# Layer norm sums that begin on VectorE and run under the weight blocks, taps written out, and earlier attention steps, in a three-layer block on one core

## The chip, the cores and the metric

The kernel runs on one core of a Trainium2 chip. The metric is the device time of one execution in microseconds (us), the median of three runs. TensorE is called PE, VectorE DVE, ScalarE ACT, GpSimd POOL and SyncE SP, as in the profile.

## The reference

A stream x of 256 rows and 2048 channels passes a convolution layer, a gated linear recurrence (HGRN), a sliding-window attention and a feed-forward layer. The change touches the first and the third. Of the convolution layer this is computed (`E` = 2048, 31 taps):

```python
def conformer_conv(h, w_in, dw, dw_b, ln_g, ln_b, w_out):
    u = h @ w_in
    a, b, z = jnp.split(u, 3, axis=-1)
    v = a * jax.nn.sigmoid(b)
    v = depthwise_conv(v, dw) + dw_b          # 31 taps along the rows, channel by channel
    v = jax.nn.silu(layer_norm(v, ln_g, ln_b))
    return (v * jax.nn.silu(z)) @ w_out
```

The layer norm takes mean and variance over the 2048 channels of a row. The attention has 32 query heads of 64 channels and 4 key and value heads, rows in two blocks of 128, a window of 128 rows, and a learned sink in each head's softmax.

## The kernel before, in words

**Weights.** All products run over weight blocks: 656 blocks of 256 x 512 fp32, loaded by SP into four slots `raw`. ACT rounds a block into `w_hi` (line 637), DVE (line 977) or POOL (line 345) subtracts to get `w_lo`, and PE then makes 12 products 128x512 with it (lines 376 to 378: hi by hi, lo by hi, hi by lo, for two 128-row halves of the block and two row blocks of x). With four slots ACT can round block n only when PE has used block n - 4. POOL makes the `w_lo` of blocks 16 to 95, because DVE is then busy with the taps.

**Order.** Each engine has its own program in which `stream` walks the blocks of a phase. `Hooks` is a table written by hand: after block i of the phase (on PE after its products, on ACT after its `w_hi`, on DVE after its `w_lo`) the engine does the steps that were put at tick i. Semaphores join the engines. The phases that matter here are `conv_ab` (4 groups of 16 blocks, 0 to 63), `conv_z` (32 blocks), `conv_out` (32), and later `kv_q` (40) and `att_out` (32), whose ticks are counted on from `kv_q` as 40 and up.

**Convolution.** For each group j of 512 channels, ACT moves a and sigmoid(b) to `atok` and `sg`, POOL multiplies them (`v_out`), PE turns the result (`v_turn`), ACT copies it into the padded `vpad` (`pad_copy`), and DVE does 31 taps for each of four channel tiles of 128 channels (`taps`, line 1032; 124 instructions a group, in a hardware loop over j). Each tap waits for the tap before the last one, since two tiles alternate.

**Layer norm.** After the last block of `conv_z`, PE turns the last quarter of z (`z_turn(3)`), adds the channels with 16 products by a matrix of 1/2048 (`mean`, line 435), DVE subtracts the mean, ACT squares, PE adds with 16 more products (`variance`, line 442), ACT takes the root, DVE the reciprocal (line 1057), and then scaling, SiLU, the gate by z, `y_hi` and `y_lo` follow for four quarters of the channels. The first product of `conv_out` needs the first `y_lo`.

**Attention.** The 32 heads go in four groups g of 8. With e = 16 + 8g: q is normalised and rotated on DVE (`rope`), turned on PE (`q_turn`), scored on PE in two halves of four heads (`scores`), masked on DVE (`masked`, line 1306), the row maxima are taken for all eight heads at once (`maxima`, lines 1313 to 1321), ACT takes the exponentials (`exps`, lines 901 and 902), PE turns the probabilities (`turn_p`, line 557), ACT copies them (`p_copy`), PE multiplies by v (`mix_v`, lines 566 to 568), DVE scales (`finish`), PE turns again (`y_turn`), and ACT and DVE make `y_hi` and `hy_lo` (`y_out_hi`, `y_low`). Block 52 on PE needs `hy_lo` of group 3.

## Time and profile before

| what | value |
|---|---|
| median of three runs | 2094.3 us (2093.97 to 2095.67) |
| the profiled execution, its own time | 2096.97 us |
| its span | 2095.2 us |
| PE busy | 2016.1 us, 96% |
| DVE busy | 1264.4 us, 60% |
| ACT busy | 1064.5 us, 51% |
| POOL busy | 203.3 us, 10% |
| granted clock of PE, mean | 0.982 of full |

The span is the part that the trace covers; the time of the execution holds 1.8 us more. A busy PE here is one with a product under way; how fast it goes is seen in the clock and in the distance from one start to the next.

### The profile page before, as it was taken

How to read it: one execution, taken by the hardware profiler on the slowest of the kernel's cores; microseconds unless marked ns; L12 is line 12 of the kernel's file. 1: busy time of each engine (PE TensorE's matmuls, PEld its weight loads, DVE VectorE, ACT ScalarE, POOL GpSimd, SP SyncE). 2: the span in 40 equal slices, each digit the busy share in tenths (PEclk: the TensorE clock that was granted, in tenths of full speed). 3: DMA queues.
4: the chain of work that ended last, by engine and by line, in shares of the span. 5: the costliest groups of instructions: out<-in, count | busy, mean ns of one | idle time of the engine just before them, and what ended most of it. 6: DMA issues, size and time to landing. Idle time of an engine off the chain costs nothing.

```text
span 2095.2 us, 26893 instructions
## 1 busy us (share of the span) xinstructions
PE 2016.1 (96%) x9504; PEld 1677.0 (80%) x9504; DVE 1264.4 (60%) x1694; ACT 1064.5 (51%) x1350; POOL 203.3 (10%) x92
## 2 busy tenths in 40 slices
PE   7999997999999999999999987999999999999999
PEld 6777776888888888878887776788888888888887
DVE  5499965543877777795657653454544545444443
ACT  6444445455758585874555553454444434443332
POOL 0888840000000000000000000000000000000000
PEclk9999998999999999999999997999999999999999
DMA  8565542566545454545564332465666665666664
GB/s 287 180 181 180 173 150 91 186 196 182 159 140 163 131 172 138 161 131 171 168 205 131 101 100 71 157 194 171 201 190 190 190 190 172 199 195 194 194 192 161
DMA packets 182855, 352.81 MB, mean 168 GB/s; under 512 B 11616, under 2 KB 12000, under 8 KB 182752
## 3 DMA queue, kind: packets, MB, share of 16 engines
q1 hardware_dynamic: 181184, 350.27, 54.5%
q10 hardware_dynamic: 1568, 1.23, 0.2%
q8 instruction: 57, 0.93, 0.2%
q14 instruction: 46, 0.38, 0.1%
HBM read 349.36 MB, written 2.10 MB: 168 GB/s over the span
## 4 chain that ended last, share of the span: by engine, by line
PE 87%; DVE 5%; ACT 4%; issue 2%; DVEq 1%; POOL 0%; ACTq 0%; DMA 0%; SPq 0%
PE acc L376 26%; PE acc L378 26%; PE acc L377 26%; PE T L477 3%; PE T L358 2%; ACT w_hi L637 1%; DVEq L969 1%; DVE w_lo L977 1%; PE T L557 1%; POOL w_lo L345 0%; PE T L566 0%; PE T L567 0%; PE T L568 0%; PE T L435 0%; PE T L487 0%
## 5 line engine op out<-in xcount | busy, mean ns | idle before, releaser
L977 DVE TENSOR_TENSOR w_lo<-raw,w_hi 128x1024 fp32r<-128x1024 f32 x576 | 699.8, 1224 | 635.6 <-ACT w_hi L637 627.7
L637 ACT ACTIVATE w_hi<-raw 128x1024 fp32r<-128x1024 f32 x656 | 683.1, 1058 | 548.0 <-PE acc L378 519.2
L376 PE MATMUL acc<-w_hi,h_hi 128*128 128x512 f32 x1888 | 748.3, 396 | 23.3 <-DVE h_lo L989 13.4
L378 PE MATMUL acc<-w_hi,h_lo 128*128 128x512 f32 x1888 | 739.3, 392 | 0.0
L377 PE MATMUL acc<-w_lo,h_hi 128*128 128x512 f32 x1888 | 739.0, 391 | 0.0
L376 PEld LDWEIGHTS acc<-w_hi,h_hi 128*128 128x128 f32 x1888 | 357.2, 189 | 99.2 <-DVE h_lo L989 13.4
L378 PEld LDWEIGHTS acc<-w_hi,h_lo 128*128 128x128 f32 x1888 | 356.7, 189 | 75.3
L377 PEld LDWEIGHTS acc<-w_lo,h_hi 128*128 128x128 f32 x1888 | 357.0, 189 | 71.2
L345 POOL TENSOR_TENSOR w_lo<-raw,w_hi 128x1024 fp32r<-128x1024 f32 x80 | 189.7, 2405 | 84.0 <-ACT w_hi L637 84.0
L1032 DVE SCALAR_TENSOR_TENSOR T<-vpad,feat,T 128x256 f32<-128x256 f32 x464 | 183.6, 483 | 0.7 <-DVE T L1032 0.6
L376 PE MATMUL acc<-w_hi,y_hi 128*128 128x512 f32 x384 | 157.3, 410 | 20.5 <-DVE y_lo L982 11.3
L377 PE MATMUL acc<-w_lo,y_hi 128*128 128x512 f32 x384 | 154.4, 402 | 0.0
L376 PE MATMUL acc<-w_hi,f_hi 128*128 128x512 f32 x352 | 137.1, 389 | 0.0
L378 PE MATMUL acc<-w_hi,f_lo 128*128 128x512 f32 x352 | 137.0, 389 | 0.0
L377 PE MATMUL acc<-w_lo,f_hi 128*128 128x512 f32 x352 | 137.0, 389 | 0.0
L376 PEld LDWEIGHTS acc<-w_hi,y_hi 128*128 128x128 f32 x384 | 75.3, 196 | 39.3 <-DVE y_lo L982 12.1
L378 PE MATMUL acc<-w_hi,hy_lo 128*128 128x512 f32 x256 | 103.4, 404 | 0.0
L810 ACT ACTIVATE E<-E 128x2048 f32<-128x2048 f32 x32 | 61.4, 1920 | 62.2 <-DVE E L1155 62.1
L377 PEld LDWEIGHTS acc<-w_lo,y_hi 128*128 128x128 f32 x384 | 75.1, 196 | 15.2
L378 PEld LDWEIGHTS acc<-w_hi,f_lo 128*128 128x128 f32 x352 | 66.1, 188 | 13.8
L377 PEld LDWEIGHTS acc<-w_lo,f_hi 128*128 128x128 f32 x352 | 66.1, 188 | 13.7
L376 PEld LDWEIGHTS acc<-w_hi,f_hi 128*128 128x128 f32 x352 | 66.1, 188 | 13.5
(196 smaller groups left out, 1379.5 us busy)
## 6 DMA issues: line engine op xcount, KB each, us to landing
raw<-in_hgrn_w_in_dram SPq DMA_DIRECT2D x160, 512.0 KB, 3.7
raw<-in_conv_w_in_dram SPq DMA_DIRECT2D x96, 512.0 KB, 4.3
raw<-in_ffn_w_gate_dram SPq DMA_DIRECT2D x88, 512.0 KB, 4.3
raw<-in_ffn_w_up_dram SPq DMA_DIRECT2D x88, 512.0 KB, 4.0
raw<-in_ffn_w_down_dram SPq DMA_DIRECT2D x88, 512.0 KB, 4.8
raw<-in_attn_w_qkv_dram SPq DMA_DIRECT2D x40, 512.0 KB, 4.3
raw<-in_conv_w_out_dram SPq DMA_DIRECT2D x32, 512.0 KB, 4.7
raw<-in_hgrn_w_out_dram SPq DMA_DIRECT2D x32, 512.0 KB, 5.1
```

The lines of the kernel that those rows point to most:

```text
L345: nc.gpsimd.tensor_tensor(w_lo[:, slot, :, :], raw[:, slot, :, :], rounded(w_hi[:, slot, :, :]), ALU.subtract).then_inc(split_ready, 1)
L358: last = nc.tensor.transpose(dst[:, q // 2, at:at + P], src[:, tb, q * P:(q + 1) * P], ident[:, :])
L376: nc.tensor.matmul(o, hi[:, kt, a], w_hi[:, slot, kk, :], start=kt == 0, stop=False)
L377: nc.tensor.matmul(o, hi[:, kt, a], w_lo[:, slot, kk, :], start=False, stop=False)
L378: last = nc.tensor.matmul(o, lo[:, kt, a], w_hi[:, slot, kk, :], start=False, stop=kt == p.chunks * CK - 1)
L477: last = nc.tensor.matmul(o, g, q, start=True, stop=True)
L557: last = nc.tensor.transpose(T[:, h % 2, b * P:(b + 1) * P], sm[:, h, b * P:(b + 1) * P], ident[:, :])
L637: A(w_hi[:, slot, :, :], raw[:, slot, :, :], ACT.Copy).then_inc(hi_ready, 1)
L810: A(e, e, ACT.Exp).then_inc(g_E, 1)
L969: return nc.vector.drain()
L977: TT(w_lo[:, slot, :, :], raw[:, slot, :, :], rounded(w_hi[:, slot, :, :]), ALU.subtract).then_inc(split_ready, 1)
L1032: STT(out=flat(cy[:, kt, :]) if tap == TAPS - 1 else y, in0=v, scalar=w, in1=y, op0=ALU.mult, op1=ALU.add).then_inc(c_tap, 1)
```

## The change

It has four parts. In the first, the taps are no longer in a loop but written out for all four groups, `v_out` of group 0 moves from POOL to DVE, the turns come at tick 4 (tick 2 for group 0) in place of 5, POOL's other `v_out` one block earlier, and the accumulators of the taps use one PSUM bank (`T[:, 2]`) in place of two.

```diff
-                if n >= 16 and n % 16 == 3 and n < 80:
+                if n >= 32 and n % 16 == 2 and n < 80:
                     v_out(n // 16 - 1)
...
-                    stream("conv_ab", j, h_hi, h_lo, Hooks().put(5, lambda: v_turn(j - 1)))
+                    stream("conv_ab", j, h_hi, h_lo, Hooks().put(2 if is_first(j - 1) else 4, lambda: v_turn(j - 1)))
...
-                return Hooks().put(2, lambda: b_out(j)).put(6, lambda: pad_copy(j))
+                return Hooks().put(2, lambda: b_out(j)).put(5 if is_first(j) else 6, lambda: pad_copy(j))
...
-                    kt = bass.ds(4 * j + 2 * half + q, 1)
-                    v = flat(vpad[:, kt, tap:tap + S])
-                    w = flat(feat[:, kt, tap:tap + 1])
-                    y = T[:, 2 + half, q * S:(q + 1) * S]
+                    kt = 4 * j + 2 * half + q
+                    v, w = vpad[:, kt, tap:tap + S], feat[:, kt, tap:tap + 1]
+                    y = T[:, 2, q * S:(q + 1) * S]
                     if i == 0:
                         dve.wait_ge(c_pad, 2 * (j + 1))
+                    if j or i >= 2:
+                        dve.wait_ge(c_tap, j * GROUP_TAPS + i - 1)
...
-            with dve.Fori(0, 4) as j:
+            def v_out(j):
+                dve.wait_ge(c_a, j + 1)
+                dve.wait_ge(c_sg, j + 1)
+                TT(atok[:, :, :], atok[:, :, :], sg[:, :, :], ALU.mult).then_inc(c_v, 1)
+            v_out(0)
+            for j in range(4):
                 taps(j)
```

In the second, DVE adds the four tiles of a group into one (`blocks_sum`) after its taps, so that PE's `mean` is 4 products, at tick 22 of `conv_z`, and `variance` is 4 products of sums that DVE makes of the squares, at ticks 25 to 28. ACT squares at ticks 27 and 28 and takes the root at tick 30.

```diff
-                for half in range(2):
-                    pe.wait_ge(c_tap, 3 * GROUP_TAPS + (half + 1) * HALF_TAPS)
-                    for kt in (range(14), range(14, KT))[half]:
-                        last = nc.tensor.matmul(T[:, 2, 0:S], ones[:, :], cy[:, kt, :], start=kt == 0, stop=kt == KT - 1)
+                pe.wait_ge(c_sum, 4)
+                for q in range(4):
+                    last = nc.tensor.matmul(T[:, 3, 0:S], ones[:, :], flat(sq[:, :, :])[:, q * S:(q + 1) * S], start=q == 0, stop=q == 3)
                 last.then_inc(c_mean, 1)
 
...
-            at = Hooks().put(5, lambda: v_turn(3))
+            def variance(q):
+
+                pe.wait_ge(c_sqsum, q + 1)
+                nc.tensor.matmul(T[:, 2, 0:S], ones[:, :], (ln_std, ln_rstd)[q % 2][:, :], start=q == 0, stop=q == 3).then_inc(c_var, 1)
+            at = Hooks().put(4, lambda: v_turn(3))
             for k in range(3):
                 at.put(8 * k + 12, lambda k=k: z_turn(k))
+            at.put(22, mean)
+            for q in range(4):
+                at.put(25 + q, lambda q=q: variance(q))
             stream("conv_z", 0, h_hi, h_lo, at)
-            z_turn(3)
-            mean()
-            variance()
-            stream("conv_out", 0, y_hi, y_lo, x_turns("conv_out", 1, (c_zc, 8)), lambda c: pe.wait_ge(c_lo, c // 2 + 1))
+            stream("conv_out", 0, y_hi, y_lo, x_turns("conv_out", 1, (c_zc, 8)).put(1, lambda: z_turn(3)),
+                   lambda c: pe.wait_ge(c_lo, c + 1))
...
+            def ln_square(q):
+                act.wait_ge(c_d, q + 1)
+                if q == 3:
+                    act.wait_ge(c_sqsum, 1)
+                A(flat((atok, fg, sq)[q % 3]), flat(cy[:, 4 * q:4 * q + 4, :]), ACT.Square).then_inc(c_sq, 1)
+
+            def ln_root():
+                act.wait_ge(c_var, 4)
+                A(ln_std[:, :], T[:, 2, 0:S], ACT.Sqrt, bias=eps[:, 0:1]).then_inc(c_std, 1)
...
+            def blocks_sum(dst, blocks, done):
+                V.tensor_reduce(dst, blocks.rearrange("p k s -> p s k"), AX.X, ALU.add).then_inc(done, 1)
...
+                dve.wait_ge(c_tap, (j + 1) * GROUP_TAPS)
+                blocks_sum(flat(sq[:, :, :])[:, j * S:(j + 1) * S], cy[:, 4 * j:4 * j + 4, :], c_sum)
...
+            def squares_sum(q):
+                dve.wait_ge(c_sq, q + 1)
+                if q >= 2:
+                    dve.wait_ge(c_var, q - 1)
+                blocks_sum((ln_std, ln_rstd)[q % 2][:, :], flat((atok, fg, sq)[q % 3]).rearrange("p (k s) -> p k s", s=S), c_sqsum)
```

In the third, the steps after the root work on eighths (`unit`) and not quarters of the channels, spread over the first ticks of `conv_out`, and `z_turn(3)` moves to tick 1 there.

```diff
-            at = Hooks().put(3, layer_norm).put(4, lambda: ln_hi(1)).put(4, lambda: ln_act(2)).put(5, lambda: ln_hi(2))
-            at.put(5, lambda: ln_act(3)).put(6, lambda: ln_hi(3))
+            at = Hooks().put(0, lambda: ln_act(0)).put(3, lambda: z_out(3)).put(5, lambda: z_copy(3))
+            for u in range(8):
+                if u < 7:
+                    at.put(u, lambda u=u: ln_act(u + 1))
+                at.put(u + 1, lambda u=u: ln_hi(u))
             stream("conv_out", 0, at.with_(x_norm("conv_out", 1)))
...
+            centre()
+            for q in range(4):
+                squares_sum(q)
+            ln_rate()
+            ln_scale(0)
+            ln_scale(1)
+            at = Hooks()
+            for u in range(8):
+                at.put(u, lambda u=u: ln_gate(u))
+                if u < 6:
+                    at.put(u, lambda u=u: ln_scale(u + 2))
+                at.put(u + 1, lambda u=u: ln_lo(u))
             dve.wait_ge(split_ready, ph["conv_out"].chunk0)
             stream("conv_out", 0, at.with_(x_norm("conv_out", 1)))
```

In the fourth, attention's steps move two ticks earlier on PE (`scores` at e + 6 and e + 7, `turn_p` from e + 8), `maxima` and `exps` wait for four heads and not eight, and in group 3 `turn_p` and `mix_v` are spread over ticks 48 to 51, where before all eight steps stood at tick 50.

```diff
-                at.put(e + 6, lambda g=g: q_turn(g))
+                at.put(e + 4, lambda g=g: q_turn(g))
                 if g:
-                    at.put(e + 7, lambda g=g: y_turn(g - 1))
-                at.put(e + 8, lambda g=g: scores(g, 0)).put(e + 9, lambda g=g: scores(g, 1))
+                    at.put(e + 5, lambda g=g: y_turn(g - 1))
+                at.put(e + 6, lambda g=g: scores(g, 0)).put(e + 7, lambda g=g: scores(g, 1))
                 for i in range(4):
-
-                    at.put(e + 10 + i if g < 3 else e + 10, lambda g=g, i=i: turn_p(g, i))
-                    at.put(e + 11 + i if g < 3 else e + 10, lambda g=g, i=i: mix_v(g, i))
+                    at.put(e + 8 + i, lambda g=g, i=i: turn_p(g, i))
+                    at.put(min(e + 9 + i, 51), lambda g=g, i=i: mix_v(g, i))
...
+            def exps(g, i):
+                act.wait_ge(a_m, 2 * g + i // 2 + 1)
+                for h in (2 * i, 2 * i + 1):
...
-                    at.put(e + 13, lambda g=g: p_copy(g, 0)).put(e + 13, lambda g=g: exps(g, 3, 6))
-                    at.put(e + 14, lambda g=g: p_copy(g, 1)).put(e + 14, lambda g=g: exps(g, 6, 8))
-            at.put(52, lambda: exps(3, 0, 8))
-            for i in range(4):
-                at.put(53, lambda i=i: p_copy(3, i))
+                    at.put(e + 8, lambda g=g: y_out_hi(g - 1))
+                if g >= 0:
+                    for i in range(4):
+                        at.put(e + 10 + i, lambda g=g, i=i: exps(g, i))
+                    for i in range(4):
+                        at.put(e + 11 + i, lambda g=g, i=i: p_copy(g, i))
...
+                m, sink = (ast[:, r, :].rearrange("p (a b) -> p a b", a=2)[:, :, h] for r in (2, 3))
+                V.tensor_reduce(m[:, 0, :], sm[:, h, 0:P], AX.X, ALU.max)
+                V.tensor_reduce(m[:, 1, :], sm[:, h, P:3 * P], AX.X, ALU.max)
+                settle()
...
                 if g > 0:
-                    at.put(e + 8, lambda g=g: finish(g - 1)).put(e + 10, lambda g=g: y_low(g - 1))
+                    at.put(e + 6, lambda g=g: finish(g - 1)).put(e + 8, lambda g=g: y_low(g - 1))
                 if g >= 0:
-                    at.put(e + 10, lambda g=g: masked(g, 0)).put(e + 11, lambda g=g: masked(g, 1)).put(e + 11, lambda g=g: maxima(g))
-            at.put(53, lambda: finish(3)).put(54, lambda: y_low(3))
+                    for half in range(2):
+                        at.put(e + 8 + half, lambda g=g, half=half: masked(g, half))
+                        at.put(e + 8 + half, lambda g=g, half=half: maxima(g, half))
+            at.put(54, lambda: finish(3)).put(54, lambda: y_low(3))
```

On DVE the place is the start of the taps of group 0 (`T` is the accumulator, `vpad` the padded input, `feat` the taps' weights). Before:

```order
L977 TENSOR_TENSOR w_lo<-raw,w_hi 128x1024 x6
L1045 UNCONDITIONAL_BRANCH
L1045 ISA
L1029 ISA x2
L1029 TENSOR_SCALAR T<-vpad,feat 128x256
L1029 ISA x2
L1029 TENSOR_SCALAR T<-vpad,feat 128x256
L1031 ISA
L1032 ISA
L1032 SCALAR_TENSOR_TENSOR T<-vpad,feat,T 128x256
L1031 REGISTER_ALU
L1032 ISA
```

After:

```order
L971 TENSOR_TENSOR w_lo<-raw,w_hi 128x1024 x6
L1045 TENSOR_TENSOR atok<-atok,sg 128x1024
L1024 TENSOR_SCALAR T<-vpad,feat 128x256 x2
L1026 SCALAR_TENSOR_TENSOR T<-vpad,feat,T 128x256 x58
L1026 SCALAR_TENSOR_TENSOR cy<-vpad,feat,T 128x256 x2
L1024 TENSOR_SCALAR T<-vpad,feat 128x256 x2
L1026 SCALAR_TENSOR_TENSOR T<-vpad,feat,T 128x256 x58
L1026 SCALAR_TENSOR_TENSOR cy<-vpad,feat,T 128x256 x2
L1030 TENSOR_REDUCE sq<-cy 128x256
```

The branch, the loop's registers and the stand-alone waits are gone, the product of `atok` and `sg` stands ahead of the taps, and a reduction of `cy` into `sq` follows each group's 124 taps.

On PE the place is the layer norm, whose sums over channels multiply by `ones`. Before, at the end of `conv_z`:

```order
L378 MATMUL acc<-w_hi,h_lo 128x512
L358 MATMUL T<-ident,sg 128x128 x8
L435 MATMUL T<-cy,ones 128x256 x16
L442 MATMUL T<-atok,ones 128x256 x4
L442 MATMUL T<-sg,ones 128x256 x4
L442 MATMUL T<-atok,ones 128x256 x4
L442 MATMUL T<-sg,ones 128x256 x4
L376 MATMUL acc<-w_hi,y_hi 128x512
L377 MATMUL acc<-w_lo,y_hi 128x512
```

After, at tick 22 of `conv_z`, between two blocks of weights:

```order
L378 MATMUL acc<-w_lo,h_hi 128x512
L379 MATMUL acc<-w_hi,h_lo 128x512
L435 MATMUL T<-sq,ones 128x256 x4
L377 MATMUL acc<-w_hi,h_hi 128x512
L378 MATMUL acc<-w_lo,h_hi 128x512
L379 MATMUL acc<-w_hi,h_lo 128x512
```

The 16 products of the mean have become 4, and they and the variance's have left the gap between the two phases.

On PE again, group 3 of attention in `att_out` (`sm` holds probabilities, `PT` their turned copy). Before, in a row at tick 50, after the last product of its block:

```order
L378 MATMUL acc<-w_hi,hy_lo 128x512
L557 MATMUL T<-ident,sm 128x128 x6
L566 MATMUL T<-kvtok,PT 128x64
L567 MATMUL T<-kvtok,PT 128x64
L568 MATMUL T<-kvtok,PT 128x64
L566 MATMUL T<-kvtok,PT 128x64
L567 MATMUL T<-kvtok,PT 128x64
L568 MATMUL T<-kvtok,PT 128x64
L557 MATMUL T<-ident,sm 128x128 x6
L566 MATMUL T<-kvtok,PT 128x64
L567 MATMUL T<-kvtok,PT 128x64
```

After, from the last product of block 51 to the last step but a few of the group:

```order
L379 MATMUL acc<-w_hi,hy_lo 128x512
L563 MATMUL T<-kvtok,PT 128x64
L564 MATMUL T<-kvtok,PT 128x64
L565 MATMUL T<-kvtok,PT 128x64
L563 MATMUL T<-kvtok,PT 128x64
L564 MATMUL T<-kvtok,PT 128x64
L565 MATMUL T<-kvtok,PT 128x64
L554 MATMUL T<-ident,sm 128x128 x6
L563 MATMUL T<-kvtok,PT 128x64
L564 MATMUL T<-kvtok,PT 128x64
```

Three of the four pairs of turn and mix have left for the ticks ahead, with 12 products of a block between them, and one pair and a half stands before the last turn.

## Rows read from the trace of the kernel before

**Rows 1.** The page, busy time of each engine and the chain by engine
```profile
PE 2016.1 (96%) x9504; PEld 1677.0 (80%) x9504; DVE 1264.4 (60%) x1694; ACT 1064.5 (51%) x1350; POOL 203.3 (10%) x92
...
PE 87%; DVE 5%; ACT 4%; issue 2%; DVEq 1%; POOL 0%; ACTq 0%; DMA 0%; SPq 0%
```

**Rows 2.** Windows: busy time of PE, PEld, DVE, ACT, POOL; clock; DMA
```profile
295.80:353.70 57.90, 41.81 (x170) 34.02 (x170) 29.97 (x25) 29.60 (x39) 0.00 (x0) 0.85 0.23 74
1251.30:1299.70 48.40, 36.73 (x163) 29.79 (x162) 16.63 (x23) 16.00 (x47) 0.00 (x0) 0.68 0.17 52
```

**Rows 3.** Timeline of ACT, two weight blocks in a row
```profile
256.11 1.06 ACT L637 ACTIVATE w_hi<-raw 128x1024 fp32r<-128x1024 f32 x1 [1.66 <-PE acc L378]
258.83 1.06 ACT L637 ACTIVATE w_hi<-raw 128x1024 fp32r<-128x1024 f32 x1 [1.66 <-PE acc L378]
```

**Rows 4.** Timeline of DVE, the taps: first, middle, last
```profile
78.71 0.99 DVE L1029 TENSOR_SCALAR T<-vpad,feat 128x256 f32 x2 [27.11 <-ACT vpad L694]
...
104.28 22.90 DVE L1032 SCALAR_TENSOR_TENSOR T<-vpad,feat,T 128x256 f32<-128x256 f32 x58
...
284.99 0.87 DVE L1032 SCALAR_TENSOR_TENSOR cy<-vpad,feat,T 128x256 f32 x2
```

**Rows 5.** Timeline, the first turn on PE and its copy on ACT
```profile
76.22 1.03 PE L358 MATMUL T<-ident,atok 128*128 128x128 f32 x8
...
77.29 1.09 ACT L694 ACTIVATE vpad<-T 128x512 f32<-128x512 f32 x2 [7.91 <-PE T L358]
```

**Rows 6.** Groups of DVE by form: busy us, mean ns, idle before
```profile
L1175 DVE TENSOR_REDUCE ssh<-E 128x8 f32<-128x1024 f32 x4 | 4.9, 1220 | 30.0 <-ACT E L830 30.0
...
L998 DVE TENSOR_TENSOR x<-acc,x 128x512 f32<-128x512 f32 x32 | 20.6, 686 | 13.3 <-PE acc L378 13.3
```

**Rows 7.** Timeline of DVE, four scalar operations without waits
```profile
998.89 1.66 DVE L989 SCALAR_TENSOR_TENSOR h_lo<-T,feat,h_hi 128x256 fp32r<-128x256 f32 x4
```

**Rows 8.** Waits of PE for POOL, and the timeline at one of them
```profile
PE acc L376 <- POOL w_lo L345: 7.5, 4, 1.9
...
128.49 0.60 PE L376 MATMUL acc<-w_hi,h_hi 128*128 128x512 f32 x1 [1.91 <-POOL w_lo L345]
```

**Rows 9.** Timeline, the layer norm: sum, reciprocal, first product, x turn
```profile
299.24 8.76 PE L435 MATMUL T<-cy,ones 128*128 128x256 f32 x32
...
318.11 1.75 DVE L1057 RECIPROCAL ln_rstd<-ln_std 128x256 f32<-128x256 f32 x1 [5.47 <-ACT ln_std L747]
...
328.06 0.80 PE L376 MATMUL acc<-w_hi,y_hi 128*128 128x512 f32 x1 [10.49 <-DVE y_lo L982]
...
361.78 1.04 PE L358 MATMUL T<-ident,x 128*128 128x128 f32 x8
```

**Rows 10.** Timeline of PE, attention: first waits of groups 0 and 1
```profile
1138.17 0.55 PE L557 MATMUL T<-ident,sm 128*128 128x128 f32 x3 [3.42 <-ACT sm L902]
...
1179.23 0.55 PE L557 MATMUL T<-ident,sm 128*128 128x128 f32 x3 [3.42 <-ACT sm L902]
```

**Rows 11.** Timeline of PE, one pair of mix and turn, and the block behind
```profile
1230.51 0.33 PE L566 MATMUL T<-kvtok,PT 128*128 128x64 f32 x2
...
1232.37 0.47 PE L376 MATMUL acc<-w_hi,y_hi 128*128 128x512 f32 x1
```

**Rows 12.** Timeline, attention group 3 and the wait before it
```profile
1247.91 0.50 PE L376 MATMUL acc<-w_hi,y_hi 128*128 128x512 f32 x1 [2.01 <-DVE hy_lo L982]
...
1257.96 1.95 DVE L1306 SCALAR_TENSOR_TENSOR sm<-T,wmask 128x384 f32<-128x384 f32 x4 [1.47 <-PE T L545]
...
1264.12 1.22 DVE L977 TENSOR_TENSOR w_lo<-raw,w_hi 128x1024 fp32r<-128x1024 f32 x1
...
1265.10 0.68 PE L557 MATMUL T<-ident,sm 128*128 128x128 f32 x3 [3.42 <-ACT sm L902]
...
1287.62 0.78 PE L376 MATMUL acc<-w_hi,y_hi 128*128 128x512 f32 x1
...
1295.85 0.60 PE L376 MATMUL acc<-w_hi,y_hi 128*128 128x512 f32 x1 [2.01 <-DVE hy_lo L982]
```

More of the change, by code:

```diff
@@ L190, in build @@
         xT = szt
+        sq = sb(conv_s, "sq", [P, TB, GC])
         ln_std = sb(conv_s, "ln_std", [P, S])
@@ L249, in build @@
         c_a, c_sg, c_v, c_T, c_pad, c_tap = (sem(f"conv_{s}") for s in ("a", "sg", "v", "T", "pad", "tap"))
-        c_z, c_zT, c_zc, c_mean, c_d, c_sq, c_var, c_std, c_n, c_act, c_g, c_hi, c_lo = (
-            sem(f"ln_{s}") for s in ("z", "zT", "zc", "mean", "d", "sq", "var", "std", "n", "act", "g", "hi", "lo"))
+        c_z, c_zT, c_zc, c_sum, c_mean, c_d, c_sq, c_sqsum, c_var, c_std, c_n, c_act, c_g, c_hi, c_lo = (
+            sem(f"ln_{s}") for s in ("z", "zT", "zc", "sum", "mean", "d", "sq", "sqsum", "var", "std", "n", "act", "g", "hi", "lo"))
         g_raw, g_T, g_act, g_lb, g_D, g_E, g_G, g_mm, g_S = (
@@ L732, in z_copy, with ln_act, ln_hi @@
                       ACT.Copy).then_inc(c_zc, 1)
+            def ln_square(q):
[6 more added lines that the diff above has]
+                A(ln_std[:, :], T[:, 2, 0:S], ACT.Sqrt, bias=eps[:, 0:1]).then_inc(c_std, 1)
+            def ln_act(u):
+                act.wait_ge(c_n, u + 1)
+                for kt in (2 * u, 2 * u + 1):
+                    last = A(cy[:, kt, :], cy[:, kt, :], ACT.Silu, scale=feat[:, kt, R_LNG:R_LNG + 1], bias=feat[:, kt, R_LNB:R_LNB + 1])
+                last.then_inc(c_act, 1)
+            def ln_hi(u):
+                act.wait_ge(c_g, u + 1)
+                A(y_hi[:, 2 * u:2 * u + 2, :], cy[:, 2 * u:2 * u + 2, :], ACT.Copy).then_inc(c_hi, 1)
             at = v_steps(3)
@@ L735, in _ @@
                 at.put(8 * k + 10, lambda k=k: z_out(k)).put(8 * k + 15, lambda k=k: z_copy(k))
+            for q in range(4):
+                at.put(27 + q // 2, lambda q=q: ln_square(q))
+            at.put(30, ln_root)
             stream("conv_z", 0, at)
[L738 to L762 removed]
+            at = Hooks().put(0, lambda: ln_act(0)).put(3, lambda: z_out(3)).put(5, lambda: z_copy(3))
[3 more added lines that the diff above has]
+                at.put(u + 1, lambda u=u: ln_hi(u))
             stream("conv_out", 0, at.with_(x_norm("conv_out", 1)))
@@ L1054, in layer_norm, with ln_scale, ln_gate, ln_lo @@
                 for q in range(4):
-                    TT(block_of(q), block_of(q), T[:, 2, 0:S].unsqueeze(1).to_broadcast([P, 4, S]), ALU.subtract).then_inc(c_d, 1)
+                    block = cy[:, 4 * q:4 * q + 4, :]
+                    TT(block, block, T[:, 3, 0:S].unsqueeze(1).to_broadcast([P, 4, S]), ALU.subtract).then_inc(c_d, 1)
+            def ln_scale(u):
+                TT(unit(u), unit(u), ln_rstd[:, :].unsqueeze(1).to_broadcast([P, 2, S]), ALU.mult).then_inc(c_n, 1)
+            def ln_gate(u):
+                dve.wait_ge(c_zc, u + 1)
+                dve.wait_ge(c_act, u + 1)
+                TT(unit(u), unit(u), szt[:, 2 * u:2 * u + 2, :], ALU.mult).then_inc(c_g, 1)
+            def ln_lo(u):
+                dve.wait_ge(c_hi, u + 1)
+                low(y_lo[:, 2 * u:2 * u + 2, :], unit(u), y_hi[:, 2 * u:2 * u + 2, :], c_lo)
+            def squares_sum(q):
[3 more added lines that the diff above has]
+                blocks_sum((ln_std, ln_rstd)[q % 2][:, :], flat((atok, fg, sq)[q % 3]).rearrange("p (k s) -> p k s", s=S), c_sqsum)
+            def ln_rate():
                 dve.wait_ge(c_std, 1)
@@ L1058, in layer_norm @@
                 settle()
[L1059 to L1075 removed]
+            centre()
+            for q in range(4):
+                squares_sum(q)
[8 more added lines that the diff above has]
+                at.put(u + 1, lambda u=u: ln_lo(u))
             dve.wait_ge(split_ready, ph["conv_out"].chunk0)
```

87 lines of the change are left out of this document (16 added, 71 removed).

## The prediction

> **What bounds the kernel now.** I read the page first. PE is busy for 96% of the span and holds 87% of the chain that ended last [rows 1], so only three things on PE can pay: waits, products that are not weight blocks, and a lowered clock. Then the windows of the two places that the change touches. The 57.9 us around the layer norm, from the end of `conv_z` to the ninth block of `conv_out`, have PE busy for 41.8 at 0.85 of the clock, and the 48.4 us of the last attention group 36.7 at 0.68 [rows 2]. Last the timelines inside. One block takes PE 2.72 us, the distance of two roundings on ACT, which follow PE's release of a slot [rows 3]. Eight blocks are 21.8 us, so the layer norm window holds 36 us that are no weight block: at its end PE waits 10.5 us for the first `y_lo`, and the 16 products of the mean (32 passes in the row) alone take 8.8 [rows 9]. POOL's `w_lo` makes PE wait 7.5 us in four places, since ACT stands waiting for a turn (7.9 us at the first one [rows 5]) while it should round; after the one shown the next product takes 0.60 us and not 0.39 [rows 8].
>
> **Part one, taps and turns.** Each turn moves one block ahead, so ACT rounds again 2.72 us earlier. The waits on POOL were 1.9 us each [rows 8], shorter than that, and I take them as gone.
>
> The first turn stood at 76.2 us behind six blocks [rows 5]; behind three it stands at 76.2 - 3 x 2.72 = 68.1. Taps began 2.5 us after it (78.7) [rows 4], so they begin at 70.6. The product of `atok` and `sg` moves to DVE at some 1.2 us (1024 elements, as `w_lo` in [rows 12]), in DVE's idle 27 us ahead of the taps [rows 4], and costs nothing; if that cover were gone it would cost those 1.2.
>
> Writing the taps out saves what the loop costs and not more. A run of 58 taps took 22.90 us, 0.393 each [rows 4]. Four operations of the same kind and size, with neither a wait nor a register between them, took 1.66 [rows 7]. The last one is some 0.48, as two taps take 0.87 [rows 4]: (1.66 - 0.48) / 3 = 0.39. So the engine sets the distance, not the register work. A group is 120 x 0.393 + 2 x 0.99 = 49.1 us, four are 196.5. Before, they took from 78.7 to 285.9, 207.2 [rows 4]: the loop cost 10.7.
>
> **Part two, the sums.** DVE reduces 1024 elements in 1.22 us where they lie in a row [rows 6]. The new reductions read with 1 KB from each element to the next, which no row shows. The bounds are 1.22 from that row and twice that; a gain against 1.22 is excluded, since the elements are as many. I take 1.22. Four come behind the taps: 4.9 us. The last sum is ready at 70.6 + 196.5 + 4.9 = 272.0.
>
> When would PE ask for it? The second group of `conv_ab` began six blocks ahead of the first turn, 76.2 - 16.3 = 59.9 [rows 5]. Tick 22 of `conv_z` is 71 blocks and six turns later, a turn some 0.9 net: 59.9 + 193.1 + 5.4 = 258.4. So the early place of the mean does not hide it: PE will wait 13.6 us there, and part one's gains on PE go into that wait. The end is set by DVE. What counts in this stage is that the blocks behind it (nine) now run beside the squares, the root and the scaling.
>
> The mean is 4 products in place of 16: 8.76 / 4 = 2.2 us [rows 9], and 3.4 at half clock, which I take, because the 10.5 us of idle before the first product of `conv_out` left it at 0.80 us in place of 0.39 [rows 9]. End 275.5. Nine blocks, 24.5; one turn, 0.9; four products of the variance at 8.76 / 16 = 0.55, 2.2; rest of the half clock 1.5, by the same first product and its followers. ACT's squares and DVE's four reductions come in time: from the mean DVE has four subtractions of some 1.15, ACT takes some 1.1 a square (the size of a rounding [rows 3]), and PE asks for the first sum three blocks (8.2 us) later. `conv_z` ends at 304.6.
>
> **Part three, the eighths.** ACT takes the root behind the 29th block, DVE's reciprocal is 1.75 [rows 9], and the scaling and SiLU of one eighth follow under three blocks (8.2 us). I put the first product's wait at 2 us (bounds 0 and 5). Then DVE sets the pace: `w_lo`, and three operations of 128x512 that are 0.69 long [rows 6]. The next starts some 0.09 before the end of one, as the scalar operations do, so a tick is 1.13 + 3 x 0.60 = 2.95 for 2.72 on PE. The ninth block starts at 304.6 + 2 + 7 x 2.95 + 2.7 = 330, and the turn of x two blocks on at 338.1, three with its own. Before it stood at 361.8 [rows 9]: **-23.5 us**.
>
> **Part four, attention.** From group 0 to group 1 the same wait comes back after 1179.23 - 1138.17 = 41.06 us; 3.42 and 0.33 of it are waits for the exponentials [rows 10]. From `masked` of the second half to the release behind the maxima DVE takes 1264.12 - 1257.96 = 6.2 us [rows 12]. With the maxima of four heads it is some 4.5, and it stands behind the first half, while `turn_p` stands two blocks behind the scores as before. So the exponentials start some 6 us earlier against the turns. But now ACT has, within four ticks, exponentials, `p_copy`, `q_out` of the next group, two table loads. Gain bounded by 0 and 3.75 of waits; I take 2 removed, and for the clock no change. Three groups: -6. The wait of 2.01 ahead of block 48 goes, as `y_turn` stands two blocks earlier, and with it some 1.5 of half clock (its product took 0.50 and those behind it more): -3.5 [rows 12].
>
> Group 3 is the largest term. From the first turn (1265.1) to block 51 (1287.6) PE makes eight steps in a row, each waiting for ACT: 22.5 us, behind a wait of 3.42 [rows 12]. After, three of the pairs lie between blocks, where a pair costs 1232.37 - 1230.51 = 1.9 us [rows 11], and one and a half stay: three pairs 5.6, the last turn, copy and mix 2.0 beyond. 22.5 + 3.4 - 7.6 = 18.3 saved. But `y_turn(3)` had block 51 as cover between the mix and itself; now `finish` is bare, one operation of 1.2 and two small ones: +1.8. Block 51 itself ran at half clock, from 1287.6 to the turn near 1292.8 (5.2 for 2.9): 2.3 saved. The chain behind the last turn (2.0 us of wait at 1295.85 [rows 12]) stays. -18.8.
> Sum: **-28.3**.
>
> **Sum.** -23.5 - 28.3 = -51.8 against the profiled execution, 2096.97 to 2045.2. It stands 2.7 above the median of the runs, so 2094.3 - 51.8 = 2042.5; I say **2043**.
>
> **The skill.** The Trainium skill, page "Advanced Engine Details and Errata", section "Memory Cachelines", says that SBUF needs at least two hits on a 16-byte line to hide its access time, and that an access pattern with another line each time is slower. It speaks against the reductions. No row of before has such a pattern. It gives no figure; at my upper bound it would make 2048 of 2043.
>
> **Rivals.** (a) The reductions cost double or more, since each element lies 1 KB from the last: 4 x 1.22 more, 2048; at four times the cost 2058. Only the four behind the taps count. For: the stride. Against: nothing measured. Chance 0.2, beside the others.
> (b) Attention only moves its waits: exponentials of two heads, `p_copy` and `q_out` in one queue make PE wait in each tick, and each idle spell brings the half clock (0.68 of the clock in the last group [rows 2]). The -6 becomes 0 and the -18.8 becomes -14: 2054. 0.15.
> (c) The taps written out run faster than 0.393, say 0.36: the last sum comes 16 us earlier, PE no longer waits, and the stage is bound by blocks, 13.6 us earlier: 2029. Against: [rows 7]. 0.05.
> (d) Slower than before: the taps' waits sit in the instructions themselves now, and if each held its engine until the tap before it had ended, the distance were its 0.48 plus some 0.06, 0.15 more. 480 x 0.15 = 72 us: 2115. It decides from 0.11 us more a tap (52 / 480). Against: each waits for the tap before the last, 0.79 us back. 0.04.
> (e) PE's clock falls less after the long wait, and attention loses nearly all its waits: 2036. 0.16.
>
> **How the numbers follow.** The forecast, 2038 to 2047, has 0.40. The range goes from 2031 to 2058, with (a), (b), (e) in it; (c), (d) and the worst of (a) are outside. Faster by over 0.2% (4 us; about what a measurement of this kernel tells from none): all but (d) and a little, 0.94. Same 0.01, slower 0.05.
>
> **What the profile will show.** Waits of PE for POOL gone; taps from 70.6, at 0.39 each, no gap but a reduction of 1.2 between the groups; one wait of PE of some 14 us for DVE's last sum near 258; the first `y_hi` product near 307; no run of eight steps in group 3. I am wrong if the taps' distance moves, if a reduction is over 1.5, or if PE waits in each tick of attention.

## The result, and the profile after

The changed kernel takes 2038.88 us (median of four runs, 2038.43 to 2039.37) beside 2094.84 for the kernel before: a ratio of 0.973, interval 0.9717 to 0.9743. The profiled execution took 2038.43, where the sum of the terms gave 2045.2. The median lies 4.1 us under the 2043 of the forecast and 0.9 us above the lower end of its 2038 to 2047. The page of the changed kernel, busy time of each engine and the chain by engine, for [rows 1]:

```profile
span 2036.6 us, 25846 instructions
...
PE 1981.5 (97%) x9456; PEld 1650.6 (81%) x9456; DVE 1283.6 (63%) x1735; ACT 1065.4 (52%) x1356; POOL 201.4 (10%) x91
...
PE 77%; DVE 14%; ACT 5%; issue 2%; DVEq 1%; ACTq 0%; DMA 0%; SPq 0%
```

PE has 48 passes fewer (9456 for 9504; two a product, 12 products each of the mean and the variance), and DVE holds 14% of the chain for 5%; the page's chain by line gives the taps (L1026) 9% of the span. The two windows of [rows 2], now:

```profile
272.50:330.00 57.50, 55.77 (x241) 45.11 (x242) 43.97 (x46) 40.10 (x56) 11.99 (x5) 0.96 0.42 136
1215.10:1241.70 26.60, 22.44 (x131) 19.29 (x130) 12.81 (x18) 13.72 (x40) 0.00 (x0) 0.89 0.39 130
```

The first window now runs from the mean at tick 22 of `conv_z` to the ninth block of `conv_out`, so it holds nine blocks more than the one of before, which began behind `conv_z`. PE is busy for 55.8 of 57.5 us at 0.96 of the clock, where it was 41.8 of 57.9 at 0.85. The second window has ticks 48 to 51 of the last attention group and the start of block 52, as the one of before: 26.6 us for 48.4. The difference, 21.8, is near the 21.9 of the ledger below, but not for the same work: the scores (two times 1.7 us) have left the window, and the wait ahead of block 48 never was in it. All waits of PE by releaser (us in total, times, longest):

```profile
PE T L435 <- DVE sq L1030: 15.1, 1, 15.1
PE acc L377 <- DVE h_lo L983: 12.9, 1, 12.9
PE acc L377 <- DVE w_lo L971: 7.1, 8, 3.9
PE T L563 <- ACT PT L911: 5.2, 5, 1.5
PE T L474 <- DVE E L1181: 4.4, 4, 1.4
PE acc L377 <- DVE hy_lo L976: 2.0, 1, 2.0
PE T L359 <- DVE apad L1356: 1.9, 1, 1.9
PE acc L377 <- DVE y_lo L976: 1.4, 1, 1.4
PE T L441 <- DVE ln_std L1030: 0.3, 1, 0.3
```

POOL is gone from this list, and so are the exponentials (`sm`); one wait of 15.1 us for DVE's last sum is new. The timeline of DVE and PE through the convolution, for [rows 4, 9]:

```profile
69.04 0.99 DVE L1024 TENSOR_SCALAR T<-vpad,feat 128x256 f32<-128x256 f32 x2 [7.47 <-ACT vpad L690]
...
69.94 22.80 DVE L1026 SCALAR_TENSOR_TENSOR T<-vpad,feat,T 128x256 f32<-128x256 f32 x58
...
117.95 2.04 DVE L1030 TENSOR_REDUCE sq<-cy 128x256 f32<-128x1024 f32 x1
...
270.58 1.89 DVE L1030 TENSOR_REDUCE sq<-cy 128x256 f32<-128x1024 f32 x1
...
272.52 3.78 PE L435 MATMUL T<-sq,ones 128*128 128x256 f32 x8 [15.11 <-DVE sq L1030]
...
275.74 0.99 PE L377 MATMUL acc<-w_hi,h_hi 128*128 128x512 f32 x1
...
305.89 0.51 PE L377 MATMUL acc<-w_hi,y_hi 128*128 128x512 f32 x1 [1.44 <-DVE y_lo L976]
...
337.20 1.03 PE L359 MATMUL T<-ident,x 128*128 128x128 f32 x8
```

Places that both traces have give the ledger, as start after less start before:

| place | shift, us | step since the last |
|---|---|---|
| ACT's rounding ahead of `b_out(0)` (57.44 before, 56.22 after) | -1.2 | -1.2, the first loads |
| turn of x in `conv_out` (361.78, 337.20) | -24.6 | -23.4, convolution |
| turn of the keys, first of attention's (1096.37, 1070.85) | -25.5 | -0.9, recurrence |
| `y_turn(2)` (1244.86, 1203.29; less two ticks of 2.72) | -36.1 | -10.6, groups 0 to 2 |
| `y_turn(3)` (1292.80, 1234.74) | -58.1 | -21.9, group 3 |
| third turn of x behind it (1346.99, 1288.41) | -58.6 | -0.5 |

The first step is no work of the change: ACT waited 0.5 us less for the first load (7.17 for 7.67), and 0.7 less ahead of its sixth rounding (20.86 for 22.08). Among the runs below that have the same code up to there, DVE's product of `atok` and `sg` starts anywhere from 59.91 to 61.20.

### The profile page after: what moved, and what is told of

The parts are those of the page before. It is cut to its first block, busy times and chain, and to the rows that moved or that the text cites. A ratio compares the mean times of both kernels' runs of the same rounds, so it can differ in the third digit from the quotient of the medians.

```text
span 2036.6 us, 25846 instructions
## 1 busy us (share of the span) xinstructions
PE 1981.5 (97%) x9456; PEld 1650.6 (81%) x9456; DVE 1283.6 (63%) x1735; ACT 1065.4 (52%) x1356; POOL 201.4 (10%) x91
## 3 DMA queue, kind: packets, MB, share of 16 engines
q10 hardware_dynamic: 1568, 1.23, 0.2%
## 4 chain that ended last, share of the span: by engine, by line
PE 77%; DVE 14%; ACT 5%; issue 2%; DVEq 1%; ACTq 0%; DMA 0%; SPq 0%
PE acc L377 23%; PE acc L379 23%; PE acc L378 23%; DVE T L1026 9%; PE T L474 3%; PE T L359 2%; ACT w_hi L633 1%; DVE w_lo L971 1%; DVEq L963 1%; ACT sm L900 0%; DVE T L1024 0%; PE T L484 0%; PE T L483 0%; PE T L554 0%; ACT E L808 0%
## 5 line engine op out<-in xcount | busy, mean ns | idle before, releaser
L378 PEld LDWEIGHTS acc<-w_lo,h_hi 128*128 128x128 f32 x1888 | 355.8, 188 | 70.6
L1026 DVE SCALAR_TENSOR_TENSOR T<-vpad,feat,T 128x256 f32<-128x256 f32 x464 | 182.5, 482 | 0.0
L378 PEld LDWEIGHTS acc<-w_lo,f_hi 128*128 128x128 f32 x352 | 66.1, 188 | 13.6
L379 PEld LDWEIGHTS acc<-w_hi,f_lo 128*128 128x128 f32 x352 | 66.1, 188 | 13.6
```

Source lines behind the costliest of these rows:

```text
L378: nc.tensor.matmul(o, hi[:, kt, a], w_lo[:, slot, kk, :], start=False, stop=False)
L379: last = nc.tensor.matmul(o, lo[:, kt, a], w_hi[:, slot, kk, :], start=False, stop=kt == p.chunks * CK - 1)
L1026: STT(out=cy[:, kt, :] if tap == TAPS - 1 else y, in0=v, scalar=w, in1=y, op0=ALU.mult, op1=ALU.add).then_inc(c_tap, 1)
```

## The experiments

Each was timed in five rounds beside the kernel before, whose medians were 2096.0 to 2096.3 in these sessions. Every ratio below is to that kernel, with an interval of 0.0013 to 0.0015 either way, some 3 us; smaller differences are read from traces.

**conv_only** and **att_only** share the change between its halves: the first is the changed kernel without the fourth part, the second the kernel before with the fourth part alone (the diff of that part, one way and the other).

> The changed kernel with its fourth part (attention) undone. If the parts are independent, it keeps what the trace of the changed kernel shows up to the start of attention (the turn of x at 337.2 us for 361.8, and 25.5 us less at 1037 us): 2094.8 - 25.5 = 2069.3 us. If the convolution's gain depends on attention's order, or half of the gain at the end comes from somewhere else, it lies outside 2067 to 2072.

> The kernel before with only the fourth part made. Independent parts: the traces give 58.6 - 25.5 = 33.1 us to attention, so 2061.7 us; my prediction's terms gave 28.3, so 2066.5. The rival that attention only moves its waits would give 2080 or more.

conv_only: 2070.27 us, 0.9878 (0.9863 to 0.9893). att_only: 2064.84, 0.9849 (0.9835 to 0.9862). Off 2096.25 these are 26.0 and 31.4, 57.4 together, and 0.973 of 2096.25 is 56.6 off. Within the intervals the halves add. The 0.9 us of the recurrence are in conv_only too (its x turn 23.3 earlier, a turn at 1038.56 for 1062.84 24.3 earlier), so they belong to the convolution's half; I did not find their cause.

**row_sum** reads the eight reductions from four neighbours in a row, so that their sums are not those of the layer norm.

```diff
-                V.tensor_reduce(dst, blocks.rearrange("p k s -> p s k"), AX.X, ALU.add).then_inc(done, 1)
+                V.tensor_reduce(dst, blocks.rearrange("p k (a b) -> p (k a) b", b=4), AX.X, ALU.add).then_inc(done, 1)
```

> The changed kernel with the eight reductions reading four neighbours in a row and not four elements 1 KB apart, which adds other elements than the layer norm needs; counts and sizes are the same. If the stride costs, each falls from 2.05 us to the 1.22 of the reduction in a row [rows 6]; four behind the taps and, since the squares' sums are paced by DVE too, up to four more are on the path: 4 x 0.8 = 3.3 to 6 us less, 2033 to 2035.6. If a 1024 element reduction into 256 results costs 2.0 whatever the stride (rival), nothing moves: 2038.9.

2033.85 us, 0.9708 (0.9694 to 0.9721). DVE's last reduction of the taps in row_sum:

```profile
267.67 1.22 DVE L1030 TENSOR_REDUCE sq<-cy 128x256 f32<-128x1024 f32 x1
```

1.22 us, for 1.89 to 2.06 with the stride (2008 ns in the mean of four). The stride costs 0.8 us a reduction, and the span is 4.6 us shorter; 0.4 of that is an earlier start of the taps (68.61 for 69.04).

**pe_mean** takes DVE's sums of the taps away and gives PE the 16 products back, spread over four ticks.

```diff
-                pe.wait_ge(c_sum, 4)
+                pe.wait_ge(c_tap, (j + 1) * GROUP_TAPS)
                 for q in range(4):
-                    last = nc.tensor.matmul(T[:, 3, 0:S], ones[:, :], flat(sq[:, :, :])[:, q * S:(q + 1) * S], start=q == 0, stop=q == 3)
+                    last = nc.tensor.matmul(T[:, 3, 0:S], ones[:, :], cy[:, 4 * j + q, :], start=j + q == 0, stop=j + q == 6)
...
-            at.put(22, mean)
+            for j, tick in enumerate((9, 10, 13, 22)):
+                at.put(tick, lambda j=j: mean(j))
...
-                dve.wait_ge(c_tap, (j + 1) * GROUP_TAPS)
-                blocks_sum(flat(sq[:, :, :])[:, j * S:(j + 1) * S], cy[:, 4 * j:4 * j + 4, :], c_sum)
```

> The changed kernel without DVE's four sums of channel blocks: PE adds the mean with 16 products again, but 12 of them at ticks 9, 10 and 13 of conv_z, and only the last four at tick 22. If DVE's last sum sets the end of the layer norm, the four reductions (2.0 us each, 7.9 in all) leave its path: last tap some 265 us for 270.5 plus its sum, time 2038.9 - 7 = 2031 to 2032 us. If PE's work sets it (rival), the 12 products come on top at 0.27 us each, 3.3 us: 2042. If the four products in place of 16 were what pays, as the change's words say, it would be slower as well.

2031.75 us, 0.9692 (0.9679 to 0.9706). PE at tick 22:

```profile
266.08 3.08 PE L435 MATMUL T<-cy,ones 128*128 128x256 f32 x8 [2.90 <-DVE cy L1028]
```

The last four products start 6.4 us earlier (266.08 for 272.52), behind a wait of 2.9 and not 15.1. Four products in place of 16 bought nothing while PE had to wait for DVE anyway; the four reductions that made them possible cost 7 us.

**loop_taps** puts the taps back in the hardware loop, as the kernel before had them. With the loop come the two PSUM banks of the accumulators and indices from registers, and the first two instructions of each half do not wait for earlier taps. The diff shows a part:

```diff
-                    kt = 4 * j + 2 * half + q
+                    kt = bass.ds(4 * j + 2 * half + q, 1)
...
-                    y = T[:, 2, q * S:(q + 1) * S]
+                    y = T[:, 2 + half, q * S:(q + 1) * S]
...
-                    if j or i >= 2:
-                        dve.wait_ge(c_tap, j * GROUP_TAPS + i - 1)
...
-            for j in range(4):
+            with dve.Fori(0, 4) as j:
                 taps(j)
```

> The changed kernel with its taps back in the hardware loop over the groups, all else the same. My price of the loop was 10.7 us, in gaps between the halves and groups, with the distance of two taps at 0.393 us in both forms; since DVE's last sum sets the end, it comes back whole: 2038.9 + 10.7 = 2049.6, and PE's wait in conv_z grows from 15.1 to 25.8. If writing the taps out paid nothing by itself (rival: only the order of DVE's sums and PE's ticks pays), 2038.9.

2049.26 us, 0.9778 (0.9765 to 0.9791). DVE in loop_taps, end of group 0, start of group 1 and the last sum:

```profile
119.40 2.06 DVE L1030 TENSOR_REDUCE sq<-cy  x1
...
122.71 1.00 DVE L1023 TENSOR_SCALAR T<-vpad,feat 128x256 f32 x2 [1.25 <-issue]
...
123.62 1.66 DVE L1026 SCALAR_TENSOR_TENSOR T<-vpad,feat,T 128x256 f32<-128x256 f32 x4
...
125.46 21.35 DVE L1026 SCALAR_TENSOR_TENSOR T<-vpad,feat,T 128x256 f32<-128x256 f32 x54 [0.18 <-DVE T L1026]
...
279.09 1.88 DVE L1030 TENSOR_REDUCE sq<-cy  x1
```

The gaps are at the groups (1.25 us with "issue", waiting for nothing that the profile shows, and 0.18 behind the first four taps); two taps stay 0.39 apart (21.35 us for 54 is 0.395). The last sum starts 8.5 us later, and PE's wait is 23.1; 0.5 of the 8.5 are later loads (DVE's product of `atok` and `sg` at 60.88 for 60.34). By spans of the profiled executions, each the fastest of its kernel, the loop costs 8.5 us; by medians it is 10.4, and the 2049.6 that I expected was met. The intervals do not part the two. The two banks were not tried apart from the loop; that the gaps lie at the turns of the loop, with nothing waited for, speaks for the loop.

**early_turn** and **pe_mean_early** move the first turn of v one block up, in the changed kernel and in pe_mean; **turns_early**, built on pe_mean, moves the other three as well. The diff is that of turns_early; the first two have only its value for the first turn (1, and 4 on ACT).

```diff
-                    stream("conv_ab", j, h_hi, h_lo, Hooks().put(2 if is_first(j - 1) else 4, lambda: v_turn(j - 1)))
+                    stream("conv_ab", j, h_hi, h_lo, Hooks().put(1 if is_first(j - 1) else 2, lambda: v_turn(j - 1)))
...
-            at = Hooks().put(4, lambda: v_turn(3))
+            at = Hooks().put(2, lambda: v_turn(3))
...
-                return Hooks().put(2, lambda: b_out(j)).put(5 if is_first(j) else 6, lambda: pad_copy(j))
+                return Hooks().put(2, lambda: b_out(j)).put(4 if is_first(j) else 5, lambda: pad_copy(j))
```

> The changed kernel with the first turn of v one block earlier on PE (tick 1 for 2) and its copy on ACT one earlier. If DVE's last sum sets the end of the layer norm, all of DVE's taps and what follows come one block (2.72 us) sooner: PE's wait in conv_z falls from 15.1 to 12.4, the time by 2.7 us, to 2036.2. If PE's blocks set it (rival), nothing moves: 2038.9. If the turn is too early for its product on DVE (ready at 61.6 us, the turn would come at 64.1), a wait of PE shows at the turn.

> The kernel pe_mean with the first turn one block earlier as well. Its PE waited 2.9 us for the last tap, so the 2.7 us fill that wait and the lowered clock behind it (3.1 us for four products in place of 1.0) goes too: 2031.75 - 2.9 - 1.5 = 2027.3 us, with a wait for y_lo that stays near 1.4. If PE has no slack there (rival), it gives the 2.7 alone or less: 2029 to 2031.7.

early_turn: 2038.86 us, 0.9725 (0.9712 to 0.9739); pe_mean_early: 2031.62, 0.9693 (0.968 to 0.9706). Neither differs from its parent, and the gain that both expectations named did not come. DVE in early_turn, the first taps and the start of group 1:

```profile
66.74 0.99 DVE L1024 TENSOR_SCALAR T<-vpad,feat 128x256 f32<-128x256 f32 x2 [4.75 <-ACT vpad L690]
...
115.66 2.00 DVE L1030 TENSOR_REDUCE sq<-cy 128x256 f32<-128x1024 f32 x1
...
119.43 0.99 DVE L1024 TENSOR_SCALAR T<-vpad,feat 128x256 f32<-128x256 f32 x2 [1.77 <-ACT vpad L690]
```

The taps begin 2.3 us earlier (66.74 for 69.04), and 1.8 of it is lost 53 us later in a wait for the second copy. The second turn was the next limit: in the changed kernel it is ready about 1 us before DVE asks.

> The kernel pe_mean with the first turn at tick 1 and the other three at tick 2 (for 4). In early_turn and pe_mean_early DVE had idle time of 1.8 and 3.8 us ahead of group 1's taps, for the copy of its turn, and the 2.3 us won at the first group were lost there. If that second turn is the next limit, DVE now has no idle time between the groups, its last tap ends 3.8 us earlier than in pe_mean_early (261.6 for 265.4), and PE has no wait at tick 22 of conv_z: 2031.6 - 2.9 of wait and some 1.5 of lowered clock = 2027.2 us. If the end is set by something else behind the taps (rival), 2031.6.

2028.13 us, 0.9676 (0.9662 to 0.9689). DVE's last taps and PE's mean in turns_early:

```profile
260.28 0.90 DVE L1028 SCALAR_TENSOR_TENSOR cy<-vpad,feat,T 128x256 f32<-128x256 f32 x2
...
262.05 1.89 PE L435 MATMUL T<-cy,ones 128*128 128x256 f32 x8
```

No idle time between groups, no wait at tick 22, and four products in 1.89 us (3.08 behind a wait of 2.9, 3.78 behind one of 15.1). All five of its times lie below all five of pe_mean_early's.

**group3_row** puts the eight steps of attention's last group back at tick 50.

```diff
-                    at.put(e + 8 + i, lambda g=g, i=i: turn_p(g, i))
-                    at.put(min(e + 9 + i, 51), lambda g=g, i=i: mix_v(g, i))
+                    at.put(e + 8 + i if g < 3 else e + 10, lambda g=g, i=i: turn_p(g, i))
+                    at.put(e + 9 + i if g < 3 else e + 10, lambda g=g, i=i: mix_v(g, i))
```

> The changed kernel with the last attention group's four turns and four mixes at tick 50 in one row, as before; the earlier scores and the maxima of four heads stay. My term gave the spreading 18.3 us less 1.8 and some 2.3 of clock. Now the exponentials are ready long before tick 50, so the wait of 3.4 stays away, but each turn and mix still waits for ACT's copy: about 12 us more, 2051, with half of the clock behind it. If the maxima and the earlier scores brought the gain (rival), the row costs its steps' waits only for the first copies, some 4 us: 2043.

2040.93 us, 0.9735 (0.9722 to 0.9748). The ratio does not part it from the changed kernel's; its span is 2.6 us longer. I had expected 12 us, and the rival 4. PE in group3_row, start of the row, two mixes inside, and the block behind:

```profile
1221.72 0.82 PE L554 MATMUL T<-ident,sm 128*128 128x128 f32 x6
...
1226.23 0.43 PE L563 MATMUL T<-kvtok,PT 128*128 128x64 f32 x2 [1.23 <-ACT PT L911]
...
1230.06 0.43 PE L563 MATMUL T<-kvtok,PT 128*128 128x64 f32 x2 [1.61 <-ACT PT L911]
...
1235.15 0.77 PE L377 MATMUL acc<-w_hi,y_hi 128*128 128x512 f32 x1
```

The row takes 13.4 us to the next block (1221.72 to 1235.15), not 22.5 as in [rows 12], though mixes still wait for copies, up to 1.6 us. Both rows as windows, of the kernel before and of group3_row:

```profile
1265.10:1287.62 22.52, 16.28 (x72) 14.49 (x73) 1.47 (x2) 11.88 (x39) 0.00 (x0) 0.51 0.15 47
```

```profile
1221.72:1235.15 13.43, 10.34 (x73) 9.28 (x72) 3.68 (x3) 9.91 (x28) 0.00 (x0) 0.87 0.49 151
```

The same steps keep PE busy for 16.28 us at a clock of 0.51 and for 10.34 at 0.87: of the 9.1 us by which the row is shorter without being spread, 5.9 are clock and 3.2 waits. In group3_row the clock is 1.00 up to 1231.40 and 0.55 over the last 3.75 us.

**before_act_order** changes ACT's order in the last group of the kernel before and nothing else.

```diff
-            at.put(52, lambda: exps(3, 0, 8))
+            at.put(52, lambda: exps(3, 0, 2))
             for i in range(4):
                 at.put(53, lambda i=i: p_copy(3, i))
+                if i < 3:
+                    at.put(53, lambda i=i: exps(3, 2 * i + 2, 2 * i + 4))
```

> The kernel before, with ACT's order in the last attention group changed alone: each copy of turned probabilities directly behind the exponentials of two heads, where all eight exponentials stood ahead of the first copy. PE's row at tick 50 stays. If the row's length came from ACT's order (the 6.0 us wait for the first copy, with half the clock behind it), 5 to 7 us go: 2089 to 2091 on this measure of 2096. If it came from each step's own wait for its copy, as my prediction had it, the row stays at 22 us and the time at 2096.

2088.33 us, 0.9963 (0.9949 to 0.9976): 7.9 us by the medians, where I had expected 5 to 7. First the kernel before, its first mix, and then before_act_order:

```profile
1272.92 0.69 PE L566 MATMUL T<-kvtok,PT 128*128 128x64 f32 x2 [6.04 <-ACT PT L913]
```

```profile
1267.27 0.69 PE L566 MATMUL T<-kvtok,PT 128*128 128x64 f32 x2 [0.42 <-ACT PT L913]
```

A wait of 6.04 us for the copy becomes 0.42. It came from the exponentials of eight heads that stood ahead of that copy on ACT, from 1264.06 to 1271.3 us in the trace of before. The row in before_act_order as a window:

```profile
1265.07:1282.00 16.93, 16.33 (x73) 14.51 (x73) 1.46 (x2) 11.79 (x39) 0.00 (x0) 0.51 0.21 63
```

PE is busy for 16.33 of 16.93 us, and the clock is still 0.51: this run took away the wait and not the slow products. So the 6.04 us wait did not make the clock low. In both traces it is low from the first turn on, behind the wait of 3.4 us for the exponentials (0.52 over the 7.8 us from 1265.10 to that mix in the kernel before). Group 1 of the kernel before has the same wait of 3.42, and there, with a block's products behind, the clock is 0.64 over the first 4.8 us (1179.23 to 1184) and then 1.00. The rest of the 7.9 us lies behind the row, where block 51 runs at 0.62 of the clock for 0.51 and block 52's first product takes 0.50 us for 0.60.

**maxima8** takes the maxima for eight heads at once.

```diff
-                act.wait_ge(a_m, 2 * g + i // 2 + 1)
+                act.wait_ge(a_m, g + 1)
...
-                    for half in range(2):
-                        at.put(e + 8 + half, lambda g=g, half=half: masked(g, half))
-                        at.put(e + 8 + half, lambda g=g, half=half: maxima(g, half))
+                    for half in range(2):
+                        at.put(e + 8 + half, lambda g=g, half=half: masked(g, half))
+                    at.put(e + 9, lambda g=g: maxima(g))
```

> The changed kernel with the maxima taken for eight heads at once again, behind the second half of the masks, and the exponentials waiting for them; the steps' ticks stay. If the maxima of four heads bring the gain of the groups, the exponentials start some 6 us later, and PE waits for them again in all four groups, 3.4 us and 1.5 of clock each: 4 x 4.9 = 20 us more, 2059. If the two ticks between the scores and the first turn cover it (rival), under 3 us more.

2065.15 us, 0.985 (0.9835 to 0.9865), 26 us over the changed kernel, where I had expected 20. One period of attention as a window (columns as in [rows 2]), of the kernel before, of the changed one, and of maxima8:

```profile
1138.17:1179.23 41.06, 37.31 (x216) 30.99 (x216) 26.61 (x36) 25.51 (x60) 0.00 (x0) 0.96 0.36 103
```

```profile
1103.63:1141.02 37.39, 35.77 (x218) 29.65 (x216) 26.85 (x41) 25.23 (x60) 0.00 (x0) 1.00 0.37 111
```

```profile
1107.74:1151.37 43.63, 38.67 (x217) 31.43 (x217) 26.63 (x36) 25.56 (x60) 0.00 (x0) 0.93 0.33 97
```

The same products take 41.1, 37.4 and 43.6 us. The wait of 3.4 for the exponentials is back, the waits for the copies stay, and the clock falls from 1.00 to 0.93. A period is 6.2 us longer than the changed kernel's, not the 4.9 of the expectation, and four such are 25.

**best** adds two edits to turns_early: the variance's last product ahead of the turn of z, and, in attention, the second copy ahead of the third pair's exponentials.

```diff
-                at.put(25 + q, lambda q=q: variance(q))
+                at.put(min(25 + q, 27), lambda q=q: variance(q))
...
                     for i in range(4):
+                        if i == 2:
+                            at.put(e + 12, lambda g=g: p_copy(g, 1))
                         at.put(e + 10 + i, lambda g=g, i=i: exps(g, i))
-                    for i in range(4):
+                    for i in (0, 2, 3):
                         at.put(e + 11 + i, lambda g=g, i=i: p_copy(g, i))
```

> The kernel turns_early with two more edits. The variance's last product stands at tick 27 of conv_z, ahead of the turn of z at 28: its sum was ready at 278.4 us and the product came at 282.95, so the root comes some 3.7 us earlier and the 1.4 us wait of PE for the first y_lo goes. In attention ACT copies the second pair of turned probabilities ahead of the third pair's exponentials, where two table loads and those stood before the copy: the waits of 1.5 us in groups 0 to 2 go (4.8 in all). Sum: 2028.1 - 1.4 - 4.8 = 2021.9 us. Rival: the copy now makes ACT stand waiting for PE's turn, the exponentials of the third pair come late, and PE waits 1 to 2 us there in each group: 2026 to 2028.

2023.32 us, 0.9655 (0.9642 to 0.9668), the fastest here. PE's waits in best (us in total, times, longest):

```profile
PE acc L377 <- DVE h_lo L987: 13.4, 1, 13.4
PE acc L377 <- DVE w_lo L975: 7.1, 8, 3.9
PE T L476 <- DVE E L1183: 4.5, 5, 1.4
PE acc L377 <- DVE hy_lo L980: 2.0, 1, 2.0
PE T L359 <- DVE apad L1358: 1.9, 1, 1.9
PE T L556 <- ACT sm L902: 0.9, 3, 0.3
PE T L565 <- ACT PT L913: 0.6, 3, 0.3
PE T L442 <- DVE ln_std L1034: 0.3, 1, 0.3
```

The wait for `y_lo` and the 1.5 us waits for the copies are gone; small ones of 0.3 for the exponentials, in groups 0 to 2, took their place, the rival's mechanism at a quarter of its price, and the two edits gave 4.8 us where I expected 6.2.

## Why the prediction was right

The sum missed the profiled execution by 6.7 us (58.5 off for 51.8): 1.2 of loads and 0.9 of the recurrence, which it did not hold, 4.2 of attention up to `y_turn(3)` and 0.5 behind it, less 0.1 of the convolution. One slip is in the sum: 361.8 less 338.1 is 23.7, not 23.5. Of its three signs of being wrong, one came true, a reduction over 1.5 us; the number held all the same, since other terms made up for it.

**Part one.** Right. The waits on POOL are gone. Taps began at 69.04 for 70.6, by 1.2 us of earlier loads and the rest in the copy. The distance is 0.393 (22.80 us for 58), so rival (c) and rival (d), the slower one, are out. Loop_taps put the loop at 8.5 us by the traces and 10.4 by the medians, where I had 10.7.

**Part two.** The mechanism held: DVE's last sum came at 272.5 (272.0), PE waited 15.1 us (13.6), and `conv_z` ended at 304.46 (304.6). The terms inside were off and cancelled, which is luck. A reduction takes 2.0 us, not 1.22, which is rival (a) at 1.65 times the price and not at 2 or 4; row_sum shows that the stride alone makes it. The Trainium skill's rule (page "Advanced Engine Details and Errata", section "Memory Cachelines"), that another line for each element is slower, agrees with the trace: 2.05 for 1.22 us. Against these 4 x 0.78 = 3.1 us stood taps that began 1.6 earlier and took 195.5 us, not 196.5. The squares' four sums cost 0.8 more each as well, and PE's ticks 25 to 28 hid it but for a wait of 0.3. Pe_mean and loop_taps show that DVE set the end: what was taken from DVE or put on it came out of PE's wait. But only down to the next limit, which my chain had not named, the second turn; early_turn found it, and turns_early removed it.

**Part three.** Right. PE waited 1.4 us (I took 2) for the first `y_lo`, the ninth block started at 329.0 (330), and the x turn moved by 23.4 us beside the loads' 1.2 (23.5).

**Part four.** The sum was low by 4.2 (32.5 in the ledger for 28.3), and its reasons were partly wrong. For groups 0 to 2 I had taken two of 3.75 us of wait as gone and no change of the clock. The idle time of a period fell from 3.75 to 1.6, as taken; but the products also got faster, 37.31 to 35.77 us busy, 0.96 to 1.00 of the clock: 1.5 us a group that I had put at nothing. In three groups that is 4.6 us, as much as the miss, and rival (e)'s mechanism. Rival (b), that the waits stay or only move, is what maxima8 shows: there the earlier ticks, ACT's new order and the spreading together leave 5 us of the attention's 31, and 26 hang on the maxima of four heads. My text gave these only the small term.

Group 3 came out at 21.9 us for 22.3, for the wrong reason. My step was that the row takes 22.5 us because eight steps each wait for ACT, and that spreading them saves it. Group3_row has the same row and loses 2 to 3 us. At `y_turn(3)` it is 5.4 late, counting the 0.55 us by which its trace is ahead at the x turn; the bare wait of 1.9 us that the spread version has ahead of that turn is already in the 5.4. Behind it the spread version gives 2.3 us back: its block 52 runs partly at the lower clock (0.84 up to the next turn of x, and 0.80 us for its first product, where group3_row has 1.00 and 0.50). The 21.9 us divide so: 3.4 for the wait ahead of the row, 3.5 ahead of block 48 (as predicted, not tried apart), 9.1 for the row itself in its old place, with the exponentials ready and no longer all ahead of the first copy, 5.4 for the spreading, of which 2.3 is given back behind it, and the rest in block 51. The 9.1 are what I had wrong: I put down as eight waits what was one wait of 6.0 us, made by ACT's order (before_act_order got 7.9 us from the order alone), and a clock of 0.51 over the row, which the order alone did not lift. What kept the clock low is not shown. The wait of 3.4 us ahead of the row is a candidate, since group3_row has no such wait there and 1.00 of the clock, but no run takes away that wait alone.
